# Fetching each streamed weight chunk of a hybrid attention and expert kernel as two transfers, split at partition 72

## The chip, the cores and the metric

The kernel runs on one core of a Trainium2 chip. The metric is the device time of one execution, in microseconds (us). PE, DVE, ACT, POOL and SP are the tensor, vector, scalar, GpSimd and sync engines of the core; sixteen DMA engines move data between the memory of the chip and the core's own.

## The reference

One layer over 1024 tokens of width 1024, with 16 learned meta tokens put in front, all in float32: a mixer of two groups of attention heads, then a retrieval of experts for each token.

```python
proj = rmsnorm(h, ln) @ w_in            # columns: qa, ka, va | qb, kb, vb
o_a = stick_breaking_attention(qa, ka, va)          # 8 heads, strictly causal
o_b = sliding_window_sink_attention(rope(qb), rope(kb), vb, sinks)   # 8 heads on 2 kv heads
h = h + concat(rmsnorm(o_a), rmsnorm(o_b)) @ w_out
# experts: 128 x 128 keys, the 16 best for each of 8 heads
q = rmsnorm(h) @ w_query
idx, g = top 16 of the sums of two key scores, softmax of the scores
u = expert_u[idx];  act = gelu(u . t)
h = h + sum over k of (g * act) * expert_v[idx]
out = rmsnorm(h)
```

Each token takes 8 x 16 = 128 experts, and each expert is a row of 1024 words of `expert_u` and 1024 of `expert_v`, so 8 KB for each token and expert.

## The kernel before

The tokens go through the core in eight blocks of 128. After a front end that computes the first projections and the first block's attention, the kernel is one long loop over 8 blocks x 128 expert columns. For each column POOL issues one gather (line 763): 128 rows of 8 KB, one for each token of the block, into one of up to nine slots of `uv` (`r_uv`). DVE takes the dot product of the row with the token (line 1437), ACT turns it into a diagonal weight (lines 1020 and 1023), and PE adds the weighted rows to the block's sum (line 1877). When PE has used a slot, POOL may fill it again. Two columns make a group, and 64 groups a block.

The rest of the mixer's work is put between the groups. The input projection of all later tokens is cut into pieces (`PIECES`), each 256 tokens of one 128-column part of the weights; `STREAM_GROUPS` says after which group PE sums each piece (`sum_piece`, lines 1541 and 1547). The last pieces are summed in the third of the eight blocks. The weights of a piece are a chunk: 128 partitions of 4 KB, 512 KB, contiguous for each partition both in memory and on the core.

There are 49 chunks. The first 13 (`NF`) each have a home of their own and are loaded at the start. The other 36 are the streamed ones: they share two homes, `h2cur` and `stream_chunk`, later `stream_chunk` alone. SP loads two of them at the start and each of the others when PE has used the chunk that lies in the same home: it waits for `proj_summed`, calls `load_chunk` (line 497), and then stores the piece that was just summed (lines 523 to 543). All this is one queue of instructions on SP, in the order of the groups. PE waits at the first piece of a chunk, on the semaphore of the chunk's home, for 16 times the number of loads into that home so far (`chunk_loads`).

Other transfers of SP in the same stretch: loads of keys, values and queries for the attention of later blocks, the rows of the next block, stores of pieces and of finished blocks. All of the program's transfers have 128, 64 or 16 partitions on the core's side.

Of the kernel before, what the change touches and what calls it, by code (L numbers as in the profile page):

```python
# [26 lines left out]
P = 128  # L27
# [5 lines left out]
PAIRS = HEADS // 2  # L33
# [120 lines left out]
NF = len(FRONT_KINDS)  # L154
# [3 lines left out]
NH = NF + 3  # L158
SPARE = NF + 11
STB = 4  # L160
STAGED = [i for i, (m, p, tb, c) in enumerate(PIECES) if m == QB or tb]
K_PIECE = {p: i for i, (m, p, tb, c) in enumerate(PIECES) if m == KA and tb == 0}
CHUNK_END = {c: i for i, (m, p, tb, c) in enumerate(PIECES)}
CHUNK_START = {c: i for i, (m, p, tb, c) in reversed(list(enumerate(PIECES)))}
CHUNK_HOME = [c if c < NF else NF + ((c - NF) % 2 if c < SPARE else 1) for c in range(len(CHUNKS))]
# [83 lines left out]
def block_program(nc, x, meta, w_chunks, w_v, consts, rope_cs, w_out, sinks, w_query, keys_t, experts, out):  # L249
    with ExitStack() as ctx:  # L250
# [3 lines left out]
        def sem(name):  # L254
            return ctx.enter_context(nc.semaphore(name))
# [12 lines left out]
        def grid(view, a):  # L268
            return view.rearrange("p (a n) -> p a n", a=a)
# [111 lines left out]
        k_first = grid(k_first_v, PAIRS)  # L381
        stage = [stage_v[:, GW * u:GW * u + GW] for u in range(STB)]
        kb_first = r_wk[:, TOP_AT + 2 * 256 + 2 * PH * NC + 512 + 2 * K:TOP_AT + 2 * 256 + 2 * PH * NC + 512 + 4 * K]

        def chunk_home(c):

            return wchunk[CHUNK_HOME[c]]

        def chunk_loads(c):

            return sum(CHUNK_HOME[a] == CHUNK_HOME[c] for a in range(c + 1))

        def piece_sums(i, w=GW):

# [34 lines left out]
        chunk_in = [sem(f"chunk_in{i}") for i in range(NF + 2)]  # L429
        stage_out = [sem(f"stage_out{i}") for i in range(STB)]  # L430
        proj_summed, proj_kept, turn_done, rope_done = (
# [57 lines left out]
        def _(sp_eng):  # L489
            e = sp_eng  # L490
# [3 lines left out]

            def load_chunk(c):
                m, p, t0, t1 = CHUNKS[c]
                e.dma_start(chunk_home(c), w_chunks[PAIRS * m + p]).then_inc(chunk_in[CHUNK_HOME[c]], 16)

            rope_of = rope_cs.rearrange("p (a n) -> p a n", a=2)
            load_x(0)  # L500
            e.dma_start(cst[:, :], consts).then_inc(consts_in, 16)
            load_x(1)
            load_chunk(0)
            load_x(NT)
            for c in range(1, 7):
                load_chunk(c)
                load_x(c + 1)
                if c == 4:
                    e.dma_start(cs_of[:, :, :], rope_of[:, :, 0:WIN]).then_inc(tile_in, 16)
            load_chunk(7)  # L510
            e.dma_start(sinkb[:, :], sinks.partition_broadcast(P)).then_inc(side_in, 16)
            load_chunk(8)
# [7 lines left out]
            def store_piece(i):  # L520
# [8 lines left out]
                elif m != QA or tb:  # L529
                    s = STAGED.index(i)  # L530
                    of, out_ = stage[s % STB], stage_out[s % STB]
                    if m == KV and p == 0:
# [12 lines left out]
            def stored(n):  # L545

                for m in range(STB):
                    e.wait_ge(stage_out[m], 16 * sum(i < n for i in STAGED[m::STB]))

# [11 lines left out]
            for s in range(NS + 1):  # L561
                if s - 1 in PIECE_AT:
                    i = PIECE_AT[s - 1]
                    c = PIECES[i][3]
# [211 lines left out]
        def _(act):  # L776
# [48 lines left out]
            def keep_piece(i):  # L825
# [8 lines left out]
                else:  # L834
                    s = STAGED.index(i)
                    into = stage[s % STB]
                    if s >= STB:
# [632 lines left out]
        def _(pe):  # L1470
# [39 lines left out]
            def sum_piece(i):  # L1510
                m, p, tb, c = PIECES[i]
                if CHUNK_START[c] == i:
                    gate(pe, "pe", chunk_in[CHUNK_HOME[c]], 16 * chunk_loads(c))
# [466 lines left out]
```

## Time and profile before

| | us |
|---|---|
| median of the runs | 2914.44 |
| lowest and highest of 3 runs | 2912.92, 2914.83 |
| span of the profiled execution, first to last instruction | 2918.2 |

The profile has no total of its own for the profiled execution beside this span. PE is busy 76% of it, DVE 75%, POOL 45%, ACT 39%; the DMA queue that holds the gathers takes 89.6% of the sixteen DMA engines' time and moves 1073.81 MB, the queue of SP's transfers 7.3% and 79.49 MB. A line of the profile such as `L1547 PE MATMUL ps<-r_uv,stream_chunk` is one group of instructions: line of the kernel, engine, operation, and the tiles written and read, by the program's names without buffer numbers. A DMA share of 1.00 means that all sixteen engines had a packet in hand all the time.

### The profile page before, as it was taken

Reading aid. Unit: us, or ns where it says so; the run is one execution under the profiler, and the core shown is the slowest. Engines: PE = TensorE matmul, PEld = TensorE weight load, DVE = VectorE, ACT = ScalarE, POOL = GpSimd, SP = SyncE. Lnnn points to the kernel's source line nnn. Section 1 sums busy time; section 2 is a strip of 40 time slices with the busy share of each in tenths; the row PEclk is TensorE's granted clock in tenths of the full one; section 3 lists DMA queues with packets and bytes.
Section 4 is the critical chain, followed back from the end, with each engine's and each line's share of the span. In section 5 each row is a group of like instructions: output and inputs, shape, how many; then the busy total and the mean of one; then the engine's idle time right before and its main releaser. Section 6 shows DMA issues by size and latency. Waiting matters only on the chain.

```text
span 2918.2 us, 30160 instructions
## 1 busy us (share of the span) xinstructions
PE 2207.9 (76%) x9182; PEld 944.6 (32%) x9182; DVE 2182.3 (75%) x5506; ACT 1144.8 (39%) x2673; POOL 1308.8 (45%) x1126
## 2 busy tenths in 40 slices
PE   9988888788887988867877777867755775565555
PEld 7564532345333453323322232212311231111111
DVE  4179887786867867689786988779776987668555
ACT  3523277433563335632575327733212321121111
POOL 0024355443554445544565445644444444444442
PEclk9999998999999999988998899988877898777778
DMA  8279999999999999999999999999999999999997
GB/s 324 91 290 406 382 404 420 407 412 389 416 387 419 413 392 411 391 415 420 420 419 408 421 419 403 416 417 418 421 409 422 420 403 420 417 422 406 422 421 322
DMA packets 189328, 1155.22 MB, mean 396 GB/s; under 512 B 23072, under 2 KB 40416, under 8 KB 57712
## 3 DMA queue, kind: packets, MB, share of 16 engines
q0 software_dynamic: 147456, 1073.81, 89.6%
q1 hardware_dynamic: 41712, 79.49, 7.3%
q8 instruction: 74, 1.21, 0.2%
q14 instruction: 86, 0.70, 0.1%
HBM read 1138.21 MB, written 15.01 MB: 395 GB/s over the span
## 4 chain that ended last, share of the span: by engine, by line
DMA 34%; PE 26%; DVE 24%; ACT 9%; issue 5%; POOL 1%; another core or an unknown queue 0%; ACTq 0%; DVEq 0%; SPq 0%; POOLq 0%
DMA r_uv<-in_experts,r_wk 34%; PE ps L1877 12%; DVE r_uv L1437 11%; PE ps L1547 4%; ACT r_uv L1023 2%; PE ps L1795 2%; PE ps L1541 2%; ACT L1020 2%; DVE r_wk L1208 1%; DVE r_wk L1206 1%; DVE r_wk L1209 1%; ACT L784 1%; PE ps L1773 1%; POOL r_uv L763 1%; PE ps L1563 1%
## 5 line engine op out<-in xcount | busy, mean ns | idle before, releaser
L763 POOL DMA_INDIRECT r_uv<-in_experts,r_wk x1024 | 1202.8, 1175 | 1416.7 <-PE ps L1877 1207.6
L1877 PE MATMUL ps<-r_uv 128*64 128x512 f32 x4096 | 1229.8, 733 | 679.0 <-ACT r_uv L1023 662.6
L1437 DVE CUSTOM_DVE_ANT_0 r_uv<-r_uv,hnrep 128x1024 f32<-128x1024 f32 x1024 | 1255.9, 1241 | 555.9 <-DMA r_uv<-in_experts,r_wk 541.0
L1877 PEld LDWEIGHTS ps<-r_uv 128*64 128x64 f32 x4096 | 290.2, 157 | 1424.2 <-ACT r_uv L1023 955.8
L1020 ACT ACTIVATE r_wk<-r_wk 128x2 f32<-128x2 f32 x512 | 103.8, 203 | 1455.5 <-DVE r_wk L1437 1426.4
L1023 ACT ACTIVATE r_uv<-gid,r_wk 128x64 f32<-128x64 f32 x684 | 200.6, 340 | 11.6 <-ACT r_wk L1020 0.2
L1020 ACT ACT_TABLE_LOAD x138 | 177.1, 1283 | 2.4
L784 ACT ACT_TABLE_LOAD x117 | 150.1, 1283 | 6.1 <-PE ps L1753 1.8
L1547 PE MATMUL ps<-r_uv,stream_chunk 128*128 128x256 f32 x560 | 134.0, 394 | 4.7 <-DMA stream_chunk<-in_w_chunks 4.7
L1795 PEld LDWEIGHTS ps<-r_wk,r_wq 128*128 128x128 f32 x1024 | 120.2, 193 | 37.4 <-issue 36.8
L1795 PE MATMUL ps<-r_wk,r_wq 128*128 128x128 f32 x1024 | 129.3, 281 | 0.3 <-ACT r_wk L940 0.3
L1547 PEld LDWEIGHTS ps<-r_uv,stream_chunk 128*128 128x128 f32 x560 | 106.2, 195 | 50.6 <-issue 36.9
L1557 PE MATMUL ps<-r_wk 64*128 64x256 f32 (+2 forms) x384 | 110.0, 419 | 4.3 <-DMA r_wk<-lkv_dram 1.9
L1421 DVE TENSOR_TENSOR gid<-cst,r_wk 128x128 f32<-128x128 f32 x342 | 106.4, 311 | 0.0
L1023 ACT ACTIVATE r_uv<-cst,r_wk 128x64 f32<-128x64 f32 x340 | 99.7, 340 | 5.7
L714 POOL TENSOR_TENSOR r_wk<-r_wk 128x512 f32<-128x512 f32 (+1 forms) x64 | 85.0, 1328 | 31.3 <-PE ps L1569 30.6
L1563 PE MATMUL ps<-r_wk,cst 128*128 128x512 f32 (+2 forms) x184 | 99.0, 621 | 0.0
L1437 DVE DVE_READ_ACCUMULATOR2_ANT r_wk<- 128x1 f32 x1024 | 83.5, 81 | 0.0
L712 POOL COPY r_wk<-r_wk 128x256 f32<-128x256 f32 x32 | 21.0, 657 | 134.7 <-PE ps L1566 106.0
L1557 PEld LDWEIGHTS ps<-r_wk 64*128 64x128 f32 (+1 forms) x384 | 45.8, 178 | 84.5 <-issue 83.8
L1569 PE MATMUL ps<-r_wk,cst 128*128 128x512 f32 (+2 forms) x152 | 72.0, 556 | 0.0
L1208 DVE TENSOR_TENSOR r_wk<-r_wk 128x800 f32<-128x800 f32 (+1 forms) x65 | 63.5, 978 | 2.2
(181 smaller groups left out, 2206.2 us busy)
## 6 DMA issues: line engine op xcount, KB each, us to landing
r_uv<-in_experts,r_wk POOLq DMA_INDIRECT x1024
stream_chunk<-in_w_chunks SPq DMA_DIRECT2D x30, 512.0 KB
r_wk<-lkv_dram SPq DMA_DIRECT2D x36, 256.0 KB
r_uv<-in_x SPq DMA_DIRECT2D x8, 512.0 KB, 10.6
r_wo<-in_w_chunks SPq DMA_DIRECT2D x8, 512.0 KB, 11.4
r_wk<-in_x SPq DMA_DIRECT2D x8, 512.0 KB
r_wo<-in_w_out SPq DMA_DIRECT2D x8, 512.0 KB, 9.5
r_wq<-in_w_query SPq DMA_DIRECT2D x8, 512.0 KB, 6.4
```

The source lines that it names most:

```text
L763: g.indirect_dma_start(uv[:, SLOT[G], :], None, experts, bass.IndirectOffsetOnAxis(idx[b % 2][:, k:k + 1], 0)).then_inc(rows_in[SLOT[G]], 16)
L784: a.preload_act_table_set("natural_log_exp_and_others")
L1020: link(a.activation(actv[:, GRP * n:GRP * n + GRP], actv[:, GRP * n:GRP * n + GRP], ACT.Gelu))
L1023: a.activation(uv[:, SLOT[K * b + k], 0:HALF], gid[(NG * b + n) % 3][:, k % GRP, :], ACT.Copy, scale=actv[:, k:k + 1]).then_inc(diag_ready, 1)
L1208: link(v.tensor_tensor(eq, eq, ci[:, h, 0:among].unsqueeze(1).unsqueeze(1).to_broadcast(every), ALU.mult))
L1421: v.tensor_tensor(gid[m % 3][:, :, :], ident64.unsqueeze(1).to_broadcast([P, GRP, HALF]), gates[b % 2][:, GRP * n:GRP * n + GRP].unsqueeze ...
L1437: v.tensor_tensor_reduce(uv[:, slot, 0:D], uv[:, slot, 0:D], hnrep[:, k % GRP, :], 1.0, 0.0, ALU.mult, ALU.add, actv[:, k:k + 1]).then_inc ...
L1547: last = t_.matmul(piece_sums(i, width), w[:, c, :], tokens, start=c == 0, stop=c == DC - 1)
L1557: t_.matmul(bank(u, r, c0, r0=r0)[:, h, :], k[rows, 0:r], q[rows, c0:GW], start=opens, stop=False, skip_group_check=True).then_inc(lz_half ...
L1563: last = t_.matmul(bank(u, r, c0), negtri[0:r, 0:r], sp[0:r, :, c0:GW], start=False, stop=not own and rest == GW, skip_group_check=True)
L1795: last = t_.matmul(into, wq[:, c, P * h:P * h + P], hnT[:, c, :], start=c == 0, stop=c == DC - 1)
L1877: last = t_.matmul(ps[HALF * j:HALF * j + HALF, i, :], uv[:, slot, 0:HALF], uv[:, slot, D + 512 * i:D + 512 * i + 512], start=n == 0, stop ...
```

## The change

`load_chunk` issues a streamed chunk (`c >= NF`) as two transfers, one of partitions 0 to 71 and one of partitions 72 to 127, back to back on SP. Both count 16 on the same semaphore, and `chunk_loads` counts two for a streamed chunk, so PE waits for both. The first 13 chunks are loaded as before.

```diff
+SPLIT = 72
         def chunk_loads(c):
 
-            return sum(CHUNK_HOME[a] == CHUNK_HOME[c] for a in range(c + 1))
+            return sum(1 if a < NF else 2 for a in range(c + 1) if CHUNK_HOME[a] == CHUNK_HOME[c])
             def load_chunk(c):
                 m, p, t0, t1 = CHUNKS[c]
-                e.dma_start(chunk_home(c), w_chunks[PAIRS * m + p]).then_inc(chunk_in[CHUNK_HOME[c]], 16)
+                home, rows_of = chunk_home(c), w_chunks[PAIRS * m + p]
+                for p0, p1 in ((0, P),) if c < NF else ((0, SPLIT), (SPLIT, P)):
+                    e.dma_start(home[p0:p1, :, :], rows_of[p0:p1, :, :]).then_inc(chunk_in[CHUNK_HOME[c]], 16)
```

## Rows read from the trace of the kernel before

**Rows 1.** The page: span, busy time of the engines, DMA in 40 slices.

```profile
span 2918.2 us, 30160 instructions
...
PE 2207.9 (76%) x9182; PEld 944.6 (32%) x9182; DVE 2182.3 (75%) x5506; ACT 1144.8 (39%) x2673; POOL 1308.8 (45%) x1126
...
DMA  8279999999999999999999999999999999999997
```

**Rows 2.** Busy table by stretch; its first line names the columns.

```profile
core 0: us, PE busy (x) PEld busy (x) DVE busy (x) ACT busy (x) POOL busy (x), PEclk, DMA share, GB/s
0.00:75.00 75.00, 68.36 (x362) 56.01 (x363) 33.98 (x94) 27.90 (x79) 0.50 (x6) 1.00 0.83 318
75.00:180.00 105.00, 97.30 (x570) 64.37 (x569) 39.99 (x150) 45.19 (x88) 13.88 (x20) 0.95 0.33 119
...
180.00:1250.00 1070.00, 902.87 (x4007) 436.81 (x4005) 830.43 (x2141) 503.98 (x1086) 491.80 (x424) 0.93 1.00 403
1250.00:2850.00 1600.00, 1097.64 (x4128) 377.01 (x4130) 1243.49 (x3057) 555.33 (x1381) 784.09 (x660) 0.84 1.01 416
```

**Rows 3.** Line 497, 180 to 1250 us, then 0 to 180: issues, who waited.

```profile
L497 SPq DMA_DIRECT2D stream_chunk<-in_w_chunks x28: 332/333/476, 191.1 to 1171.9; - x28
L497 SPq DMA_DIRECT2D h2cur<-in_w_chunks x3: 332/332/333, 197.8 to 236.1; - x3
...
  PE ps L1547: 5.7, 3
...
L497 SPq DMA_DIRECT2D h2cur<-in_w_chunks x3: 328/328/1079, 22.2 to 155.4; - x3
...
L497 SPq DMA_DIRECT2D stream_chunk<-in_w_chunks x2: 332/960/1589, 23.3 to 140.7; - x2
```

**Rows 4.** DMA queues, 180 to 1250 us: packets, MB, share of 16 engines.

```profile
q0 software_dynamic: 54250, 395.03, 90.9%
q1 hardware_dynamic: 21600, 35.40, 8.9%
q8 instruction: 33, 0.54, 0.2%
q14 instruction: 34, 0.28, 0.1%
```

**Rows 5.** DMA queues, 1250 to 2850 us.

```profile
q0 software_dynamic: 89675, 653.06, 98.8%
q1 hardware_dynamic: 8016, 12.13, 2.1%
q8 instruction: 34, 0.56, 0.1%
q14 instruction: 47, 0.39, 0.1%
```

**Rows 6.** Waits, 180 to 1250 us: us in total, times, longest.

```profile
POOL r_uv L763 <- PE ps L1877: 490.8, 166, 11.7
...
DVE r_uv L1437 <- DMA r_uv<-in_experts,r_wk: 196.1, 169, 4.1
```

**Rows 7.** Chain of waits by line, 180 to 1250 us, then 1250 to 2850.

```profile
by line: DMA r_uv<-in_experts,r_wk 17.6%; PE ps L1877 14.1%; DVE r_uv L1437 12.1%; PE ps L1547 6.7%; issue 6.0%; PE ps L1541 4.0%; PE ps L1795 3.5%; ACT L1020 2.7%; ACT L784 2.4%; ACT r_uv L1023 2.3%; DVE r_wk L1208 1.5%; DVE r_wk L1206 1.5
...
by line: DMA r_uv<-in_experts,r_wk 47.6%; PE ps L1877 12.5%; DVE r_uv L1437 11.9%; issue 4.3%; ACT r_uv L1023 2.4%; DVE r_wk L1208 1.3%; DVE r_wk L1206 1.3%; DVE r_wk L1209 1.2%; POOL r_uv L763 1.2%; ACT L1020 1.1%; ACT r_wk L1020 0.9%; DVE
```

**Rows 8.** Chain of waits, 300 to 345 us: start, us, what.

```profile
316.73 3.78 PE ps L1541 x32
...
320.60 7.94 DMA stream_chunk<-in_w_chunks
```

**Rows 9.** Timeline of SP at one chunk load: start, us, instruction.

```profile
320.60 0.33 SPq L497 DMA_DIRECT2D stream_chunk<-in_w_chunks  x1
320.97 0.43 SPq L535 DMA_DIRECT2D vb_dram<-stage  x1
```

**Rows 10.** Waits of SP, 180 to 1250 us.

```profile
SPq L482 <- PE ps L1576: 256.8, 16, 46.0
```

## The prediction

> **What bounds the kernel now.** I read five kinds of view, in this order: the page's head, the busy table by stretch, the DMA queues of a stretch, the waits, and the chain of waits.
>
> The page's head shows no engine filled: PE is at 76%, DVE at 75%. The line that is full is DMA, nine tenths or more in 36 of the 40 slices [rows 1]. The busy table separates the stages [rows 2]. Up to 75 us the DMA engines are 0.83 busy, from 75 to 180 us 0.33: there the front end computes and the transfers wait for it. From 180 us on the share is 0.99 to 1.01. The stretch that matters is 180 to 1250 us, because 31 of the 36 streamed chunk loads are issued in it: 28 into `stream_chunk` and 3 into `h2cur` [rows 3]. The other five are issued between 22 and 155 us.
>
> In that stretch the four queues add up to 90.9 + 8.9 + 0.2 + 0.1 = 100.1% of sixteen engines [rows 4]; after it, 98.8 + 2.1 + 0.1 + 0.1 = 101.1% [rows 5]. The second sum is over 100 because neighbouring packets overlap a little in the records, so I read it as "full". Then the streaming stretch lacks 101.1 - 100.1 = 1.0%, that is 0.010 x 1070 = 10.7 us of an average engine. So the sixteen engines are the resource that is used up, in both halves. They move 403 GB/s in one and 416 in the other [rows 2]; the first carries more small packets: 21600 of the hardware queue, against 8016 in the longer second [rows 4, 5].
>
> The waits say how tight that is. POOL, which issues the gathers, waits 490.8 us in this stretch for a free slot (for PE to have used the rows), and DVE waits 196.1 us for rows that have not landed [rows 6]. In the chain of waits the gathers have 17.6% of this stretch, and 47.6% of the later one [rows 7]. So here it is a ring: a slot is filled, dotted by DVE, weighted by ACT, summed by PE and filled again, and both compute and DMA stand in the circle. A ring whose DMA station is 99% busy passes on most of what is added to that station, but not all.
>
> **What the change removes, adds and moves.** No byte is added. Each of the 36 chunk loads becomes two instructions on SP; PE's gate counts 32 in place of 16 for each load. Three things can cost.
>
> First, SP. One more issue of 0.33 us per chunk [rows 3, 9], 31 x 0.33 = 10.3 us of SP in this stretch. Behind it on SP stands the store of the piece just summed, issued at 320.97 right after the load at 320.60 [rows 9]; it would go out 0.33 us later. SP itself waits 256.8 us in this stretch for one pair of its waits alone [rows 10], so the extra issue lies inside them. POOL issues the gathers itself and isn't behind it. I cost this at 0; if the cover were gone, 10.3 us is its most.
>
> Second, when the chunk lands. PE waits for a chunk three times in the stretch, 5.7 us in all [rows 3], and one of these is on the chain of waits, 7.94 us from issue to landing at 320.60 [rows 8]. The other loads arrive before their piece. Where the busiest engine carries a quarter more of the chunk (next paragraph), landing stretches by about a quarter, 0.25 x 7.94 = 2.0 us, at three places: 0 to 6 us of PE. PE's wait can hide behind the DMA engines, which go on with gathers meanwhile, so I take 0 to 1 us of it and keep 6 for the range.
>
> Third, and this carries the forecast: how the rows are dealt over the sixteen engines. All transfers that the program now makes have 128, 64 or 16 partitions, which sixteen engines share evenly: 8 rows of a chunk for each engine. 72 and 56 are not multiples of 16, and no row of the trace of before shows such a transfer. I bound it from both sides. If rows are dealt as evenly as possible, 72 is 4 or 5 an engine and 56 is 3 or 4; where the larger shares fall on different engines the total is still 8, and nothing changes; where they fall on the same ones it is 9. If a transfer is cut in equal whole shares, 72 goes on 12 engines with 6 rows each and 56 on 14 with 4 each, and if both start from the same engine twelve of them carry 10 rows, two 4 and two none. The busiest engine then has 10 / 8 = 1.25 times its present chunk work.
>
> By the Trainium skill, page "DMA: Bandwidth & Descriptors", section "Why a DMA increments its semaphore by 16 and not by 1", a transfer issued from SP goes on the largest number of engines up to 16 that divides its outermost dimension, and on the lowest-numbered ones; that is the equal-share case, and no row here shows it.
>
> The price of a chunk on one engine comes from the queue lines [rows 4]. The gathers' queue moves 395.03 MB in 90.9% of 1070 us, 2.46 us for each MB; the hardware queue 35.40 MB in 8.9%, 2.69 us for each MB. A chunk is 0.524 MB (512 KB), so 1.29 to 1.41 us of each engine. Its packets are 4 KB rows; the gathers' queue averages 395.03 MB / 54250 = 7.3 KB and the hardware queue 35.40 MB / 21600 = 1.6 KB, and I take a value between, 1.32 us. A quarter of it is 0.33 us (0.32 to 0.35). Times 31 chunks: 10.2 us (9.9 to 10.9) more work on each of twelve engines in the streaming stretch, and on four engines less: 20 to 40 us that nobody can use, since every gather needs rows from all sixteen.
>
> How much of 10.2 us ends up in the time? Nothing if it went wholly into the 10.7 us of idle DMA time, all if none did. That idle time is there because the ring sometimes has no slot free [rows 6], not because an engine ran out of work at the end, and it will go on occurring for the same reason. But a chunk load goes out right after a piece's matmuls, which are 3.7 us on PE that no expert row gets [rows 8], so some of the added packets meet just such a moment. I let the slack take a sixth: 10.2 x 5/6 = 8.5 us, and with up to 1 us from the late chunk it is 9.
>
> The five loads before 180 us cost nothing: they meet engines that are 0.33 to 0.83 busy [rows 2], and the extra is 5 x 0.35 = 1.8 us at most.
>
> **The sum.** The profiled execution has a span of 2918.2 us [rows 1]; the runs shown have 2912.92 to 2914.83, median 2914.44, so the profiled one stands 3.8 us or 0.13% above them. I add the difference to the median: 2914.4 + 9 = 2923 us.
>
> **The rivals.** (a) No change that can be measured. Either the rows are dealt evenly (0, or with 9 rows on the busiest 0.125 x 1.32 x 31 = 5.1 us less the slack), or the ring's idle time swallows most of the 10 us. For it: 1.0% of slack is almost exactly the size of the extra work, and the chain gives gathers only 17.6% here [rows 7]. Against it: a queue that is 99% busy has its idle moments scattered. It gives 2914 to 2919. The even deal is also the case in which the change does not do anything but issue twice.
>
> (b) Faster. The mechanism: a gather counts as landed when its last engine has landed, and if that laggard is one of the four engines that lose chunk work, the other twelve no longer wait for it. The place is the streaming stretch; the price is what the others now idle, 10.7 us by the sums, up to 2.0% or 21 us if both shares of the busy table were rounded the unfavourable way [rows 2]. Against this stand the 10.2 us that the same twelve take on. So it decides for faster only if over 10 us of their idle time is waiting for one such engine; at its most 2914 - 11 = 2903 us. Nothing in the views names an engine that lags, so its chance is small.
>
> The same page, section "Latency and other measured facts", says that the engines numbered 7 and 15 are usually the slower ones; with 15 among the relieved it would speak for (b), with 7 among the loaded against it, and no row here shows engine numbers.
>
> (c) Much slower. The late chunk stops PE at its three places for the full 6 us and nothing covers it, and the slack takes nothing: 10.9 + 6 = 17 us, 2931 us. It needs the stop to empty the gathers' queue as well, which three stops can hardly do.
>
> **How the numbers follow.** A run of this kernel can tell about 0.2%, 5.8 us, from no change. The forecast (6 to 13 us slower, 2920.5 to 2927) has 0.67, (a) 0.25, (b) 0.05, (c) 0.03. That gives slower 0.70, same 0.25, faster 0.05. The range takes in the forecast, nearly all of (a) down to no change at all with the spread of the runs under it, and the lower part of (c): 2913 to 2930. Left out are (b) and the far end of (c), with some room for errors in price.
>
> **What would show it.** In the profile after, the chunk issues in 180 to 1250 us should number 62, and landing from issue should grow from under 8 us to nearly 10. If the equal shares hold, the busy share of the sixteen engines falls in the streaming stretch by about what four engines are spared, (2 x 40 + 2 x 20 - 12 x 10) / 16 = 0, no change in the work, but the stretch is 9 us longer, so GB/s and share fall by some 0.8%, and the gathers land later by about 0.3 us for each chunk that they meet. The time from 1250 us on should be unchanged, only shifted. The prediction is wrong if the streaming stretch ends at the same time as before (a deal that is even, or slack that covers it), or if it ends earlier.

## The result and the profile after

The changed kernel takes 2976.32 us in the median (2971.51 to 2977.41), the kernel before 2913.68 us in the same set of runs. The ratio is 1.0215 with a 95% interval of 1.0199 to 1.0231: 62.6 us slower, where 9 us were forecast and 2930 us was the upper end of the range. The profiled execution has a span of 2969.7 us, 51.5 us over the span before [rows 1]. That is less than 62.6 because the profiled execution of the kernel before stood above its median, and this one is the shortest of its four; readings of the profile below are of these two executions.

The page of the changed kernel: span, DMA in 40 slices, GB/s, and its two large queues (packets, MB, share of 16 engines).

```profile
span 2969.7 us, 30196 instructions
...
DMA  8289999999999999999999999999999999999997
GB/s 315 93 292 360 345 365 408 402 387 391 394 387 396 380 391 381 384 408 420 420 420 406 419 419 420 409 416 420 419 416 418 418 405 421 416 422 410 422 421 324
...
q0 software_dynamic: 147456, 1073.81, 89.3%
q1 hardware_dynamic: 42072, 79.50, 8.0%
```

The streaming stretch now ends some 55 us later: what was done from 180 to 1250 us is done from 180 to 1305 us (430.97 MB against 431.25). The busy table of the changed kernel for that stretch and for what follows, columns as in [rows 2]:

```profile
180.00:1305.00 1125.00, 919.89 (x3995) 443.03 (x3992) 829.14 (x2138) 501.76 (x1080) 502.37 (x425) 0.92 1.00 383
1305.00:2900.00 1595.00, 1105.05 (x4124) 381.20 (x4124) 1243.19 (x3056) 554.61 (x1379) 782.16 (x658) 0.83 1.01 417
```

The loss lies in the first line. The DMA share stands at 1.00 as before, but the engines move 383 GB/s in place of 403. After 1305 us the rate is that of before, 417 GB/s against 416. So in the streaming stretch the engines are as busy as before and get less done. The DMA queues of the changed kernel, 180 to 1305 us:

```profile
q0 software_dynamic: 54201, 394.75, 89.7%
q1 hardware_dynamic: 21910, 35.40, 10.1%
```

Against [rows 4] the bytes are the same, and each of them is dearer. The gathers' queue takes 0.897 x 1125 / 394.75 = 2.56 us for each MB, before 2.46; the hardware queue 0.101 x 1125 / 35.40 = 3.21 us, before 2.69. That is 395 x 0.094 = 37 us of the gathers, which the change doesn't touch, and 35.4 x 0.52 = 18 us of SP's transfers, together the 55 us by which the stretch has grown. With the share at 1.00 in both executions the two parts must add up to that; what the sum tells is how the growth divides. That packets themselves have become slower is seen in the time that the trace gives for each packet: the 4 KB packets of SP's queue, most of them rows of chunks, take 159 ns in the median before and 213 ns after. Of the gathers' 8 KB packets the median hardly moves, 309 and 311 ns, but the mean rises from 322 to 334 ns, so a part of them is slowed.

The rest of the after-profile answers to what was forecast of it. In the stretch the chunk issues (line 500, first two lines below) are 56 + 6 = 62, and PE waits for chunks 14.3 + 4.7 = 19.0 us in eight waits, before 5.7 in three [rows 3]. Three of these waits are on the chain of waits, 10.4 to 11.8 us long from issue to landing (two of them below), before one of 7.94 [rows 8]. DVE waits longer for gathers, 257.9 us against 196.1 [rows 6], and the chain of waits has gone over to DMA: 29.3% of the stretch are gathers, before 17.6% [rows 7].

```profile
L500 SPq DMA_DIRECT2D stream_chunk<-in_w_chunks x56: 299/361/651, 185.6 to 1226.4; - x56
L500 SPq DMA_DIRECT2D h2cur<-in_w_chunks x6: 300/336/864, 192.3 to 232.3; - x6
...
  PE ps L1550: 14.3, 6
  PE ps L1544: 4.7, 2
...
DVE r_uv L1440 <- DMA r_uv<-in_experts,r_wk: 257.9, 196, 5.5
...
320.13 11.79 DMA stream_chunk<-in_w_chunks
...
338.08 10.43 DMA stream_chunk<-in_w_chunks
...
by line: DMA r_uv<-in_experts,r_wk 29.3%; PE ps L1880 14.1%; DVE r_uv L1440 8.5%; PE ps L1550 7.3%; issue 5.0%; PE ps L1544 4.6%; DMA stream_chunk<-in_w_chunks 2.9%; PE ps L1798 2.8%; ACT r_uv L1026 2.1%; ACT L1023 1.9%; ACT L787 1.7%; POOL
```

One count settles how the rows are dealt. A gather is 147456 / 1024 = 144 packets: 128 rows, and one more for each of sixteen engines. The hardware queue of the kernel before has 41712 packets on its page, that of the changed kernel 42072. The difference is 360 = 36 x 10, and 10 = 12 + 14 - 16: twelve engines closed the transfer of 72 rows and fourteen that of 56, where sixteen closed the whole one. So the number of engines is that of the forecast's equal shares. How many rows each carried follows from it only if the shares are equal, and that the same twelve carry both transfers is not seen.

```profile
q1 hardware_dynamic: 41712, 79.49, 7.3%
```

(The line is of the kernel before.) This agrees with the Trainium skill, page "DMA: Bandwidth & Descriptors", section "Why a DMA increments its semaphore by 16 and not by 1", in the number of engines. Which of them they are no run shows.

### The profile page after: what moved, and what is told of

Its sections match the earlier page's. It is cut to its first block, busy times and chain, and to the rows that moved or that the text cites. A ratio compares the mean times of both kernels' runs of the same rounds, so it can differ in the third digit from the quotient of the medians.

```text
span 2969.7 us, 30196 instructions
## 1 busy us (share of the span) xinstructions
PE 2234.4 (75%) x9182; PEld 956.5 (32%) x9182; DVE 2182.6 (73%) x5506; ACT 1145.3 (39%) x2673; POOL 1318.4 (44%) x1126
## 3 DMA queue, kind: packets, MB, share of 16 engines
q0 software_dynamic: 147456, 1073.81, 89.3%
## 4 chain that ended last, share of the span: by engine, by line
DMA 39%; PE 27%; DVE 20%; ACT 8%; issue 5%; POOL 2%; SPq 0%; ACTq 0%; DVEq 0%; POOLq 0%
DMA r_uv<-in_experts,r_wk 37%; PE ps L1880 12%; DVE r_uv L1440 10%; PE ps L1550 5%; ACT r_uv L1026 2%; PE ps L1544 2%; PE ps L1798 2%; ACT L1023 2%; POOL r_uv L766 1%; DMA stream_chunk<-in_w_chunks 1%; ACT L787 1%; DVE r_wk L1209 1%; DVE r_wk L1211 1%; DVE r_wk L1212 1%; ACT r_wk L1023 1%
## 5 line engine op out<-in xcount | busy, mean ns | idle before, releaser
L1880 PE MATMUL ps<-r_uv 128*64 128x512 f32 x4096 | 1244.9, 740 | 693.5 <-ACT r_uv L1026 679.6
L1209 DVE TENSOR_TENSOR r_wk<-cst,r_wk 128x800 f32<-128x800 f32 (+1 forms) x65 | 63.4, 976 | 2.2
## 6 DMA issues: line engine op xcount, KB each, us to landing
r_uv<-in_x SPq DMA_DIRECT2D x8, 512.0 KB, 10.4
```

Source lines behind the costliest of these rows:

```text
L1209: link(v.tensor_tensor(eq, iota[:, 0:among].unsqueeze(1).unsqueeze(1).to_broadcast(every), grid(posf[:, h, cols], halves).unsqueeze(3).to_ ...
L1880: last = t_.matmul(ps[HALF * j:HALF * j + HALF, i, :], uv[:, slot, 0:HALF], uv[:, slot, D + 512 * i:D + 512 * i + 512], start=n == 0, stop ...
```

## The experiments

Three theories to begin with. A: the unequal shares, twelve engines with 10 rows of a chunk. B: rows written by engines that collide over the same part of the core's memory, which slows packets; later told apart as B1 (a transfer touches only a part of the partitions), B2 and B3 (below). C: the two issues and completions by themselves. Most kernels are the changed one with another cut in `load_chunk`; four copy rows from memory to memory besides, three of them with whole loads. In the table us are the ratio less 1, times the median of before. "Rows on the busiest engine" takes the shares to be equal and the engines to be counted from the same first one. The price of each MB in the two queues is worked out from the queue lines of 180 to 1250 us, as above (share x 1070 / MB; for the change this gives 3.23 where the longer window above gave 3.21).

| streamed chunk loaded as | rows on the busiest engine | ratio (95%) | us | us per MB, SP's queue | us per MB, gathers |
|---|---|---|---|---|---|
| 128 (before) | 8 | | | 2.69 | 2.46 |
| 72 + 56 (the change) | 10 | 1.0215 (1.0199 to 1.0231) | +63 | 3.23 | 2.56 |
| 128 + 128, half the columns each | 8 | 1.0005 (0.9996 to 1.0015) | +1 | 2.75 | 2.46 |
| 80 + 48 | 8 | 1.0143 (1.0124 to 1.0162) | +42 | 3.19 | 2.52 |
| 64 + 64 | 8 | 1.0150 (1.0131 to 1.0169) | +44 | 3.29 | 2.53 |
| 112 + 16 | 8 | 1.0101 (1.0074 to 1.0128) | +29 | 3.06 | 2.52 |
| 88 + 40 | 12 | 1.0273 (1.0245 to 1.0300) | +80 | 3.19 | 2.58 |
| half the columns whole, half 80 + 48 | 8 | 1.0069 (1.0050 to 1.0088) | +20 | 2.99 | 2.49 |
| 64 even + 64 odd | 8 | 1.0001 (0.9987 to 1.0015) | 0 | 2.72 | 2.45 |
| every 8th, eight times 16 | 8 | 1.0161 (1.0128 to 1.0193) | +47 | 3.14 | 2.54 |
| every 4th, four times 32, by half columns | 8 | 1.0063 (1.0042 to 1.0085) | +18 | 2.84 | 2.46 |
| 56 + 8 even, 56 + 8 odd | 10 | 1.0167 (1.0133 to 1.0201) | +49 | 3.11 | 2.54 |
| 48 + 16 even, 48 + 16 odd | 8 | 1.0112 (1.0088 to 1.0135) | +33 | 3.09 | 2.52 |

**Two issues, cut by columns.**

```diff
-                for p0, p1 in ((0, P),) if c < NF else ((0, SPLIT), (SPLIT, P)):
-                    e.dma_start(home[p0:p1, :, :], rows_of[p0:p1, :, :])...
+                for c0, c1 in ((0, DC),) if c < NF else HALVES:        # (0, 4), (4, 8)
+                    e.dma_start(home[:, c0:c1, :], rows_of[:, c0:c1, :])...
```

> Each streamed chunk as two transfers of all 128 partitions, each with half of the columns (2 KB a partition), in place of the cut by partitions. Sixteen engines share both evenly and each engine keeps its partitions. Theory A (twelve engines carry more rows than the others): no change against before, within 5 us. Theory B (an engine writes partitions that another engine's gathers write at the same time, and both slow down): no change, within 5 us. Theory C (two issues and two completions a chunk cost the time): +40 to +60 us, as the change itself.

Measured 1.0005: nothing. Two issues, two completions and 2 KB rows cost nothing that can be told from zero here, and theory C has fallen.

**Equal shares, cut at 80 and at 64.** The same loop with `((0, 80), (80, P))` and `((0, 64), (64, P))`.

> The same cut by partitions, but at 80: 80 is 16 x 5 and 48 is 16 x 3, so in equal shares every engine carries 8 rows of a chunk as before. Theory A: no change, within 5 us. Theory B: most of the change's cost stays, +30 to +60 us, since the rows still lie elsewhere than in a transfer of 128. Theory C: +40 to +60 us.

> The cut at 64: 4 rows for each engine in both transfers, 8 in sum. Theory A: no change, within 5 us. Theory B: a cost between 0 and that of the cut at 80, since more rows stay with the engine that had them. Theory C: +40 to +60 us.

42 and 44 us. Both kernels have 42288 packets in the hardware queue, 36 x 16 more than before, so all sixteen engines took part in both transfers, which in equal shares is 8 rows for each. Two thirds of the loss are there without any unequal share, so theory A can't be the main one. That the cut at 64 costs no less than that at 80 is against what I had expected of B. Queue lines of the cut at 80, 180 to 1250 us:

```profile
q0 software_dynamic: 52322, 381.06, 89.9%
q1 hardware_dynamic: 21824, 35.27, 10.5%
```

**Unequal work without writing to the core.** The kernel before, and behind each streamed load:

```diff
+                if c >= NF:
+                    e.dma_start(spare_dram[c - NF, :, 0:D], w_chunks[PAIRS * m + p, 0:24]...).then_inc(spare_out, 16)
```

> The kernel before with its chunk loads whole, and behind each streamed one a transfer of 24 rows of 4 KB from memory to a spare place in memory: in equal shares 2 rows more for each of twelve engines, with no writes to the core's own memory. It adds to twelve engines what the change adds to them. Theory A: the whole cost of the change, +40 to +60 us, comes with it. Theory B: only the engines' own time, 31 x 2 x 0.16 to 0.2 us, about +10 us. Theory C: +40 to +60 us, for there are two issues again.

1.0012 (0.9998 to 1.0025), 3.5 us, not clear of zero. The 36 transfers added 43008 - 41712 = 1296 = 36 x (24 + 12) packets, so twelve engines had two rows more each. This is the work that the forecast priced at 31 x 0.33 = 10.2 us, except that it adds rows where the change moves them from other engines, and writes none into the core's memory. By itself it costs a third of the price or less.

**The cut at 112 and at 88.** `((0, 112), (112, P))` and `((0, 88), (88, P))`.

> The cut at 112: 7 rows for each engine, then 1, so an equal deal of 8 again; the first transfer spreads over 112 of the 128 partitions. Theory B1 (a transfer that touches only part of the partitions crowds the engines onto a part of the memory's entrances): the cost shrinks with the share of partitions that the transfers miss, so +5 to +15 us, clearly under the 43 us of the cut at 64. Theory B2 (any row that another engine carries than in a transfer of 128 collides with the gathers, which keep their engines): +30 to +50 us, as at 80 and 64, for nearly every row has changed its engine. Theory A (unequal shares alone): no change.

> The cut at 88: 88 is 11 x 8 and 40 is 10 x 4, so in equal shares ten engines carry 12 rows, one 8 and five none. Theory B alone: about the +40 us of the equal cuts. With theory A on top (the busiest engine's share of slowed rows sets the pace): at 72 it was 10 rows and 20 us above the equal cuts, here 12 rows, so about 40 us above them, +75 to +100 us in all.

29 us at 112: more than B1 allows, a little under what B2 expects. 80 us at 88, in the window of "A on top of B": with 8, 10 and 12 rows on the busiest engine the cuts at 64 and 80, at 72 and at 88 cost 42 to 44, 63 and 80 us. The hardware queue there has 41892 packets, 36 x 5 more than before, and 5 = 11 + 10 - 16.

**Reading or writing.** The kernel before, with a second copy of each streamed chunk into the chip's memory, once whole and once cut at 64:

```diff
+                if c >= NF:
+                    for p0, p1 in ((0, 64), (64, 128)):         # the other kernel: ((0, 128),)
+                        e.dma_start(spare_dram[c - NF, p0:p1, 0:D], w_chunks[PAIRS * m + p, p0:p1]...).then_inc(spare_out, 16)
```

> The kernel before, its chunk loads whole, and behind each streamed one a second transfer of the same 128 rows from memory to a spare place in memory. It measures what 0.5 MB more for each chunk costs where all engines share it evenly: 31 x 1.3 us, about +40 us if the sixteen engines are the bound; under +15 us if the ring has the slack that the 24-row run seemed to show. It is the base for the next kernel.

> As the run before it, but the second copy is cut at row 64 into two transfers. If the slowing lies where rows are read from the chip's memory (theory D), it costs 30 to 45 us more than the uncut copy, as the cut of the real loads did. If it lies where rows are written into the core's memory (theories B1, B2), it costs the same as the uncut copy within 8 us, for the copy writes nothing there.

1.0075 (1.0047 to 1.0103) whole and 1.0074 (1.0047 to 1.0102) cut: the same 22 us. The hardware queues of the two, 180 to 1250 us, whole and then cut, and the busy table of the whole copy (columns as in [rows 2]):

```profile
q1 hardware_dynamic: 26064, 51.65, 12.5%
...
q1 hardware_dynamic: 26560, 51.66, 12.6%
...
180.00:1250.00 1070.00, 900.01 (x3968) 437.82 (x3964) 825.04 (x2125) 492.72 (x1062) 487.55 (x418) 0.93 1.01 412
```

The packets read at the same rows cost 2.59 and 2.61 us for each MB. So it isn't the reading of rows that the cut slows, and theory D has fallen; the slowing goes with writing into the core's memory. The whole copy also shows what the ring takes up: 0.524 MB more for each of 31 chunks is 31 x 1.29 to 1.41 = 40 to 44 us of every engine, and 22 us of it reach the time, about half. So a share of 1.00 is not yet the most that the engines can move in this stretch: with the copy they move 412 GB/s at a share of 1.01, before 403 at 1.00.

**No gathers in flight.** The front end's 13 chunks cut, the streamed ones whole:

```diff
-                for p0, p1 in ((0, P),) if c < NF else ((0, SPLIT), (SPLIT, P)):
+                for p0, p1 in ((0, 64), (64, P)) if c < NF else ((0, P),):      # and ((0, 80), (80, P))
```

> The 13 chunks of the front end are cut at 64, the streamed ones are whole. No gather is in flight there before 165 us. Theory B2 (the slowed rows collide with the gathers, which keep their engines): the front end's rate stays at 405 GB/s between 10 and 45 us and the time doesn't move. Theory B3 (a cut transfer puts two engines on the same part of the core's memory, by itself and beside whole transfers): the rate falls to between 250 and 350 GB/s, and the first gather is issued 2 to 10 us later.

> The same with the cut at 80. Theory B2: 405 GB/s between 10 and 45 us, no change in time. Theory B3: a lower rate, by about as much as at 64 or less, since 80 partitions are a wider target than 64.

In time both are too noisy to say much, 1.0025 (0.9994 to 1.0055) and 1.0019 (1.0001 to 1.0037). The rate is plain. Busy table of 10 to 45 us, before, cut at 64, cut at 80 (last column GB/s):

```profile
10.00:45.00 35.00, 34.54 (x202) 30.46 (x201) 19.56 (x60) 14.22 (x41) 0.00 (x0) 1.00 1.02 405
...
10.00:45.00 35.00, 33.18 (x188) 29.18 (x188) 19.95 (x61) 13.78 (x40) 0.00 (x0) 1.00 1.03 288
...
10.00:45.00 35.00, 34.27 (x199) 29.99 (x198) 19.58 (x59) 14.25 (x41) 0.00 (x0) 1.00 1.03 304
```

With the engines full (1.02, 1.03), the rate falls from 405 to 288 and 304 GB/s, with not one gather in flight. The first gather goes out at 179.93 us in the kernel cut at 64, before at 165.81, so 14 us later, more than expected (175.30 us in the kernel cut at 80; each is one execution). The gathers are not needed for the slowing: SP's own transfers slow one another, as theory B3 has it. That it is two engines at the same part of the memory is not seen.

**Half the dose.** The first half of the columns as one transfer of 128, the second half cut at 80.

> Half of the dose: of each streamed chunk the first half of the columns as one transfer of 128 partitions, the second half cut at 80. If the cost comes row by row from the bytes whose engine has changed (theories B2 and B3): about half of the 39 us of the cut at 80, +15 to +25 us. If it comes with each cut transfer, however small: +35 us and more.

20 us, half of 42: the cost goes with the bytes that are cut, not with the number of cuts.

**Even and odd partitions.** `home[p0:P:2, :, :]` for p0 = 0 and 1.

> Each streamed chunk as two transfers of the 64 even and the 64 odd partitions. Equal deal, 4 rows an engine each, and both transfers spread over the whole of the partitions. Theory B1 (the part of the partitions that one transfer misses): no cost, within 8 us. Theories B2 and B3 (the rows have other engines than in a transfer of 128): +30 to +50 us, as at 64 and 80.

1.0001: nothing, and prices of 2.72 and 2.45 us for each MB. Its queue lines, 180 to 1250 us:

```profile
q0 software_dynamic: 54356, 395.87, 90.8%
q1 hardware_dynamic: 22096, 35.40, 9.0%
```

Here B1 is right, which the cut at 112 spoke against, and B2 and B3 in the words of their expectation are wrong: two transfers of 64 rows are free, if the rows are every second one of 128.

**Range, or certain partitions.** Eight transfers in both kernels: every eighth partition, or every fourth by half columns.

> Each streamed chunk as eight transfers of 16 partitions, every eighth one: 0, 8, 16 ... 120, then 1, 9 ... and so on. Each engine has one row of each, 8 in all, and each transfer spans all of the partitions. Theory S (a transfer is free of cost when its rows are spread over the whole range of partitions): no more than the next kernel. Theory P (the engines crowd on entrances that go by certain bits of the partition's number; by the Trainium skill, page SBUF, State Buffer, section Door 1, every eighth partition reaches 8 of 16): 30 us or more above the next kernel.

> Eight transfers too, but of every fourth partition (32 of them) and half of the columns each. Two rows of 2 KB for each engine in each transfer. By the section named it reaches all 16 entrances. Theory S and theory P: within 10 us of before, the extra from smaller packets and six more issues.

47 and 18 us, 29 apart, where theory P wanted 30 or more. That every eighth partition spans the whole range doesn't help it (theory S falls); its packets are slowed as in the contiguous cuts, while the prices of every fourth stay near those of before, 2.84 and 2.46. The 18 us are more than the 10 I had allowed; the gathers' price is that of before, so they aren't slowed packets of the gathers. PE waits 20.1 us for chunks in that kernel, before 5.7; whether that is what they are is not shown. By the Trainium skill, page "SBUF — State Buffer", section "Door 1: The DMA port swizzle", partitions 0 to 63 reach 8 of the memory's 16 ports, and which port it is goes by bits 2 to 4 and 6 of the partition's number. By my estimate from that rule, every eighth partition reaches 8 too, every second and every fourth all 16. The cut at 64, the front end cut at 64, the free cut into even and odd partitions and these two runs agree with it.

**Unequal shares, spread.**

> Unequal shares without the crowding: four transfers, the even partitions 0 to 110 (56 rows, 14 engines, 4 each), the even ones from 112 (8 rows, 8 engines), and the same of the odd ones. In equal shares eight engines carry 10 rows, six 8, two none: the busiest carries as many as with the cut at 72. If unequal shares are dear by themselves: +15 to +25 us, the difference between the cuts at 72 and at 80. If they are dear only where packets are slowed (theory A on top of the crowding): +2 to +10 us.

> Four transfers with equal shares: the even partitions 0 to 94 (48 rows, 3 for each engine), the even ones from 96 (16 rows, 1 each), and the same of the odd ones. It has the spread and the four issues of the run with 56 and 8 even rows, but not its unequal shares. If unequal shares made that one dear: within 10 us of before. If it was which engine carries which partition (theory N: only cuts that leave each engine the same part of the memory as in a whole transfer are free): +30 to +50 us.

49 us and 33 us: both slow their packets (3.11 and 3.09 us for each MB), the second with equal shares and every transfer of it on all sixteen engines. So 33 of the 49 us come without unequal shares; the forecast missed because it took the spread to be free of crowding, and it was not. The other 16 us are of the size that the first expectation gives for unequal shares, 15 to 25 us, though the two kernels also differ in which partitions go together.

**The 20 us between the cuts at 72 and at 80.** The kernel cut at 80 with the 24 rows from memory to memory behind each chunk.

> The equal cut at 80, and behind it the 24 rows from memory to memory that put two rows more on each of twelve engines. If unequal shares cost 20 us once packets are slowed (theory A on top): +55 to +70 us, the time of the cut at 72. If not: +42 to +50 us, the cut at 80 plus the 3.5 us that the extra rows cost by themselves; the 20 us then come from which partitions the cut at 72 puts on which engine.

1.0168 (1.0141 to 1.0196), 49 us: the 42 of the cut and some 7 more. Two rows more on each of twelve engines don't bring the cut at 80 to the 63 us of the cut at 72. Most of the difference lies in the cut at 72 itself: its gathers' packets cost 2.56 us for each MB against 2.52, 395 x 0.035 = 14 us. This speaks against extra work on twelve engines as the cause, but not against unequal shares of the slowed rows, for the extra rows are not written into the core's memory. The cuts at 72 and 88 and the pair above, where unequal shares go with 20, 37 and 16 us more, leave that open.

**What stays open.** Shown: a whole chunk that is cut by partitions has its packets slowed, in SP's queue by 14 to 22% and in the gathers' by 2 to 5%, when the transfers write into the core's memory; neither the number of transfers, nor equal shares, nor the range spanned decides it by itself. Only the loads of all 128 partitions, of every second and of every fourth left the gathers' price as it was. Why is not shown. One account is a theory N: a transfer is free where each engine keeps the part of the memory that it has in a transfer of 128 rows, so that no two engines meet. But the profile names no engine of a packet, so N is argued and not shown.

Mere coverage is a rival that fits as well, if it is counted as the rows that fall on the fullest port in each transfer, added up over the transfers of a chunk. By the port rule of the Trainium skill, page "SBUF — State Buffer", section "Door 1: The DMA port swizzle", my estimate of that sum is 8 for the loads of all, of every second and of every fourth partition, 12 for 112 + 16, 48 + 16, 56 + 8 and the half dose, and 16 for the cuts at 64, 72, 80 and 88 and for every eighth. The price in SP's queue goes with it in all thirteen rows of the table: 2.69 to 2.84 us for each MB, then 2.99 to 3.11, then 3.14 to 3.29. So the 112 + 16 and 48 + 16 cuts, which touch nearly everything and are still slow, do not decide for N. The count was made after the runs, and none was made to test it. Nor is it shown why 72 slows the gathers more than 80.

## Why the prediction was wrong

**What bounds the kernel** held in the main: the loss is in that stretch and in the engines' time. But I read a share near 100% as full, and with the second copy the same engines moved 412 GB/s where they move 403.

**SP at 0** held: two issues by half columns cost 1 us.

**The late chunk** was sized too small: PE waits 19.0 us for chunks in place of 5.7, in eight places and not three, so 13.3 us more where 0 to 6 were allowed, and the landings on the chain take 2.5 to 3.9 us longer, not 2.0. How much of the 55 us this makes on its own isn't separated.

**The deal** held as far as it is seen: 12 and 14 engines, by the count of packets.

**The price of a chunk** is the step that failed. I took 1.32 us for a chunk on an engine from the queues before and kept it for the new transfers, and wrote that no byte is added. The bytes are the same, but not their price: the term of 0.33 us for each chunk, on which the forecast rests, was 55 / 31 = 1.8 us, of which two thirds are gathers that wait behind slowed packets or are slowed themselves. I had no bound for that at all, and the gathers' own price of 2.46 us for each MB, which became 2.56, I took as untouched. The bounds that I set were for the number of rows on the busiest engine, and the price of a row had only the spread of two queues, both made of transfers that sixteen engines share evenly.

**The slack** failed too, the other way. I let the ring swallow a sixth; the 24-row run let through 3.5 of 10.2 us and the whole second copy 22 of 40 to 44. The copy's 18 to 22 us that stay out of the time are more than the 10.7 us of idle time that I had read from the shares. With a price as I had assumed, these two runs put the change at some 3.5 to 5.5 us (an estimate), where rival (a) stood. So the direction came out as forecast by luck, through a cause that the prediction did not have: the extra rows on twelve engines, to which it gave 0.67, cost 3.5 us by themselves, and the 42 to 44 us of the equal cuts come without them. The 20 us between those and the 63 us of the change go with the unequal shares, or with which partitions the cut at 72 puts together; the runs do not tell these apart.

**The rivals**: (a) fell; the even deal of its "evenly" is the cuts at 80 and 64, which cost 42 and 44 us. (b) fell. (c) forecast 17 us, about a quarter of the measured size, and for another reason. **The test in the profile**, a rate lower by 0.8%, came out as 5%, 383 against 403 GB/s; the time after 1250 us was only shifted, as said.

## What to carry to other kernels

A load that is cut by partitions is not the same load twice. If a cut is needed, cut by columns or take every second partition: both were free here, and every cut of whole chunks into contiguous blocks of partitions cost between 29 and 80 us. Where DMA engines are full, price a change of shape by the time of a packet and not by bytes alone, for slowed packets also hold up transfers that the change doesn't touch. And a full engine share doesn't mean that work added to it reaches the time: in this ring about half of a whole second copy did.

## What the runs showed of the hardware that I had not expected

From 10 to 45 us, with no gather in flight, the front end loads at 288 GB/s when its chunks go as two transfers of 64 partitions and at 405 when they go as one of 128, although both use sixteen engines. The same cut costs nothing when the rows go from memory to memory (the copy costs 22 us whole and cut), and nothing when it takes even and odd partitions (1.0001). A transfer of 72 rows runs on twelve engines, of 56 on fourteen, of 88 on eleven and of 40 on ten, as the packet counts 360 and 180 show.
